# Decoder trunk with expert gathers on one core: three weight buffers, twenty 2 MB weight loads for twenty-three, and a gather ring of eight and then ten rows

## The reference, cut to what matters

```python
for layer in range(2):
    h = rmsnorm(x, norm_mix_g[layer])
    x = x + (hybrid_ab(h, w_in, ..., w_out) if layer == 0 else s5_block(h, ..., glu_w, glu_b))
    h = rmsnorm(x, norm_ffn_g[layer])
    x = x + peer(h, wq[layer], subkeys[layer], u_tab[layer], v_tab[layer])
out = rmsnorm(x, final_norm_g)

def peer(h, wq, subkeys, u_tab, v_tab):          # 8 heads, 128 keys twice, top 16 of 16384 experts
    q = (xt @ wq).reshape(t, 8, 2, 128)
    sc = einsum('thpc,pkc->thpk', q, subkeys)
    sv, si = top_k(sc, 16)                       # both halves, then the best 16 of 16 x 16 pairs
    idx, gate = the 16 best pairs, softmax of their scores
    act = gelu(einsum('td,tkd->tk', x, u_tab[idx]))
    return einsum('tk,tkd->td', gate * act, v_tab[idx])
```

## Time and profile before

| what | value |
|---|---|
| median of 3 runs | 1552.95 us |
| the profiled execution, its own time | 1553.37 us |
| its span | 1551.6 us |
| bytes moved | 603.39 MB, of them 536.90 by the gathers |
| busy, DVE | 1111.5 us (72%) |
| busy, PE | 1097.8 us (71%) |
| busy, ACT | 770.2 us (50%) |

### The profile page before, as it was taken

One profiled execution on the slowest core, in us unless ns is written; L12 is line 12 of the kernel. 1 busy time (PEld: TensorE's weight loads), 2 busy tenths in 40 slices (PEclk: granted clock), 3 DMA queues, 4 the chain that ended last, 5 costly groups with the idle time before them and its releaser, 6 DMA issues.

```text
span 1551.6 us, 19133 instructions
## 1 busy us (share of the span) xinstructions
PE 1097.8 (71%) x5920; PEld 348.4 (22%) x5920; DVE 1111.5 (72%) x2533; ACT 770.2 (50%) x2120; POOL 589.4 (38%) x517
## 2 busy tenths in 40 slices
PE   7997678866765666679866575656878666666665
PEld 3542222322211212223221121212323111111110
DVE  2356887479787899985477799999456866666554
ACT  2315554445456667764334666766334644444433
POOL 0024343323443354554334345344432443434430
PEclk9998689878966776879988567686998777676675
DMA  9569999999999998999999999999999999999995
GB/s 358 179 234 413 420 405 418 414 415 408 415 421 421 354 374 358 410 421 415 412 413 414 403 357 369 355 363 406 380 416 415 415 422 421 421 421 421 421 422 234
DMA packets 105418, 603.39 MB, mean 389 GB/s; under 512 B 9314, under 2 KB 9442, under 8 KB 39780
## 3 DMA queue, kind: packets, MB, share of 16 engines
q0 software_dynamic: 73728, 536.90, 84.8%
q1 hardware_dynamic: 31588, 65.26, 11.3%
HBM read 601.08 MB, written 1.05 MB: 388 GB/s over the span
## 4 chain that ended last, share of the span: by engine, by line
DMA 32%; DVE 31%; PE 22%; ACT 7%; issue 3%; DVEq 3%; ACTq 1%; POOL 1%; SPq 0%; POOLq 0%
DMA rings<-in_uv_tab_dram,idx 24%; DVE rings L1324 11%; PE ps L715 9%; PE ps L920 8%; DMA wst<-in_wq_dram 7%; DVE mem L1231 2%; PE ps L908 2%; DVE dgs L1324 2%; ACT dgs L667 1%; DVE mem L1213 1%; ACT wgt L664 1%; DMA rings<-in_w_in_dram 1%; DVE mem L1242 1%; ACT L661 1%; DVE mem L1240 1%
## 5 line engine op out<-in xcount | busy, mean ns | idle before, releaser
L920 PE MATMUL ps<-rings,dgs 64*64 64x512 f32 x3648 | 638.0, 804 | 343.3 <-ACT dgs L667 342.6
L463 POOL DMA_INDIRECT rings<-in_uv_tab_dram,idx x456 | 521.7, 1144 | 804.3 <-PE ps L920 687.8
L1324 DVE CUSTOM_DVE_ANT_0 rings<-rings,h 128x1024 f32<-128x1024 f32 x456 | 550.7, 1224 | 210.8 <-DMA rings<-in_uv_tab_dram,idx 197.7
L661 ACT ACTIVATE gel<-dots 128x1 f32<-128x1 f32 x512 | 102.1, 199 | 522.2 <-DVE dots L1324 518.5
L920 PEld LDWEIGHTS ps<-rings,dgs 64*64 64x64 f32 x3648 | 128.3, 163 | 783.4 <-ACT dgs L667 682.3
L667 ACT ACTIVATE dgs<-cst,wgt 128x128 f32<-128x128 f32 x512 | 205.6, 402 | 36.3 <-issue 1.5
L715 PE MATMUL ps<-wst,hT 128*128 128x512 f32 x320 | 168.0, 666 | 37.1 <-DMA wst<-in_wq_dram 20.5
L664 ACT ACTIVATE wgt<-gel,share 128x1 f32<-128x1 f32 x512 | 150.8, 295 | 35.5 <-issue 0.3
L920 PE MATMUL ps<-dgs 64*64 64x512 f32 x448 | 80.2, 795 | 53.2 <-ACT dgs L667 53.1
L463 POOL DMA_INDIRECT dgs<-in_uv_tab_dram,idx x56 | 65.9, 1176 | 88.3 <-PE ps L920 74.8
L715 PEld LDWEIGHTS ps<-wst,hT 128*128 128x128 f32 x320 | 63.4, 212 | 138.1 <-issue 134.9
(11 more groups left out here) (192 smaller groups left out, 991.2 us busy)
## 6 DMA issues: line engine op xcount, KB each, us to landing
wst<-in_wq_dram SPq DMA_DIRECT2D x15, 2048.0 KB, 28.2
wst<-in_w_out_dram SPq DMA_DIRECT2D x4, 2048.0 KB, 22.8
wst<-in_glu_w_dram SPq DMA_DIRECT2D x4, 2048.0 KB, 31.7
rings<-in_uv_tab_dram,idx POOLq DMA_INDIRECT x456, 15.7
rings<-in_w_in_dram SPq DMA_DIRECT2D x3, 2048.0 KB, 16.7
rings<-in_w_in_dram SPq DMA_DIRECT2D x2, 1024.0 KB, 7.5
dgs<-in_w_in_dram SPq DMA_DIRECT2D x1, 2048.0 KB, 19.4
vec<-in_vecs_dram SPq DMA_DIRECT2D x3, 512.0 KB, 17.2
```

The costliest lines, as they stand in the source:

```text
L463: nc.gpsimd.indirect_dma_start(out=ring[g % RING], out_offset=None, in_=uv_tab, in_offset=bass.IndirectOffsetOnAxis(ap=idx[n % AHEAD][:, s ...
L661: A.activation(gel[i][:, every], dots[i][:, every], ACT.Gelu_apprx_tanh)
L920: ins = PE.matmul(ps[64 * b:64 * b + 64, 4 + 2 * t + half, :], diag[rows, g % DIAGS, rows], ring[g % RING][rows, D + b * BANK:D + (b + 1) ...
L1324: V.tensor_tensor_reduce(out=u, in0=u, in1=h[:, t, :], scale=1.0, scalar=0.0, op0=ALU.mult, op1=ALU.add, accum_out=dots[n % 2][:, s:s + 1] ...
```

## The change

- A third weight buffer: the whole tile `dgs`, once z (1, 3) has read block 3 of w_in there. `BLOCK_OF` gives the block that each product reads, `BUFFER` the buffer of each block. Both w_out blocks stay in `wst` from tile 0 to tile 1, the first three quarters of wq of layer 0 go one after the other through the third buffer, and the third of them (wq block 2) stays there for both phases. 20 loads are left of 23; layer 1 has the same loads as before, through two buffers.
- `Z_ORDER`: (1, 3) stands sixth, where it stood tenth, and all of it stands in front of `w_mm` of tile 0; half of z 5 stood behind it. The other four products of tile 1 follow later.
- The ring has eight rows, all in `rings`, for g < 80, and ten (two more in `dgs`) from g = 80 on; row 88, the first in `dgs`, waits until the product (1, 2) has left the third buffer.
- Seven diagonals in a tile of their own, `dia`, for 16; ScalarE waits for `v_done` of row g - 7 before it writes one.
- `AHEAD` 8 for 16; the searches of heads 6 to 12 stand four to six slots later; the query quarters of phase 1 stand at slots 68, 74, 81, 89 for 68, 76, 84, 92, and the one of block 2 is now the second.

```diff
-RING = 9
-AHEAD = 16
+SHORT, RING = 8, 10
+SHORT_ROWS = 80
+AHEAD = 8
-DIAGS = 16
+DIAGS = 7
-Q_USE = {(0, 0): 2, (0, 1): 3, (0, 2): 4, (0, 3): 7, (1, 3): 8, (1, 0): 9, (1, 1): 10, (1, 2): 11,
+Q_USE = {(0, 0): 2, (0, 1): 3, (0, 2): 4, (0, 3): 7, (1, 3): 8, (1, 2): 9, (1, 0): 10, (1, 1): 11,
...
-SHARED_USE = 8
+BLOCK_OF = [0, 1, 2, 3, 4, 0, 1, 5, 5, 4, 6, 7] + list(range(8, 20))
+BUFFER = [0, 1, 2, 2, 2, 0, 1, 0] + [1, 0] * 6
...
-Z_ORDER = [(0, 0), (0, 1), (0, 2), (0, 4), (0, 3), (1, 0), (1, 1), (1, 2), (1, 4), (1, 3)]
+Z_ORDER = [(0, 0), (0, 1), (0, 2), (0, 4), (0, 3), (1, 3), (1, 0), (1, 1), (1, 2), (1, 4)]
...
-ROUTE_AT = {1: 0, 2: 16, 3: 26, 4: 40, 5: 50, 6: 72, 7: 80, 8: 88, 9: 96, 10: 104, 11: 112, 12: 120, 13: 134, 14: 150,
+ROUTE_AT = {1: 0, 2: 16, 3: 26, 4: 40, 5: 50, 6: 76, 7: 84, 8: 94, 9: 102, 10: 110, 11: 118, 12: 126, 13: 134, 14: 150,
...
-           ("z", 5, 0, 3), ("mix", 0), ("mix_T", 0), ("mixT_copy", 0), ("z", 5, 3, 4),
-           ("warm",), ("w_mm", 0, 0, 0, 8), ("w_sum", 0, 0), ("w_mm", 0, 1, 0, 8), ("w_sum", 0, 1), ("z", 5, 4, 8),
+           ("z", 5, 0, 4), ("mix", 0), ("mix_T", 0), ("mixT_copy", 0), ("z", 5, 4, 8), ("z_out", 5),
+           ("warm",), ("w_mm", 0, 0, 0, 8), ("w_sum", 0, 0), ("w_mm", 0, 1, 0, 8), ("w_sum", 0, 1), ("z", 6, 0, 4),
...
-    query(0, 76, 1, 0)
-    query(0, 84, 1, 1)
-    query(0, 92, 1, 2)
+    query(4, 10, 1, 2)
+    query(5, 1, 1, 0)
+    query(5, 9, 1, 1)
...
-            for m, ns in ((w_out, (0, 1)), (wq[0], (0, 1, 2)), (w_out, (0, 1)), (wq[0], (3, 0, 1, 2)), (glu_w, (0, 1)),
-                          (wq[1], (0, 1, 2, 3)), (glu_w, (0, 1)), (wq[1], (0, 1, 2, 3))):
+            for m, ns in ((w_out, (0, 1)), (wq[0], (0, 1, 2, 3, 0, 1)), (glu_w, (0, 1)), (wq[1], (0, 1, 2, 3)),
+                          (glu_w, (0, 1)), (wq[1], (0, 1, 2, 3))):
...
+                    earlier = [v for v in range(w) if BUFFER[v] == BUFFER[w]]
+                    if earlier:
+                        last_use = max(u for u in range(len(BLOCK_OF)) if BLOCK_OF[u] == earlier[-1])
                         sp.wait_ge(w_used, last_use + 1)
+                    elif BUFFER[w] == 2:
+                        sp.wait_ge(z_done, Z_ORDER.index((1, 3)) + 1)
...
-                if g < RING and g % 2 == 0:
-                    pool.wait_ge(z_done, 6 + g // 2)
-                if g >= RING:
-                    pool.wait_ge(v_done, g - RING + 1)
+                if g < SHORT and g % 2 == 0:
+                    pool.wait_ge(z_done, 7 + g // 2)
+                if row_ahead(g) >= 0:
+                    pool.wait_ge(v_done, row_ahead(g) + 1)
+                elif ring_at(g) == SHORT:
+                    pool.wait_ge(w_used, Q_USE[1, 2] + 1)
...
+                if g >= DIAGS:
+                    act.wait_ge(v_done, g - DIAGS + 1)
```

More of the change, by code:

```diff
@@ L229, in trunk @@
         wst = sb("wst", [P, 2, KC, BANK])
+        dia = sb("dia", [P, DIAGS * P])
         mem = sb("mem", [P, 9472])
@@ L272, in trunk @@
         sgb = sb("sgb", [P, 8])
-        ring = [rings[:, 2 * D * i:2 * D * (i + 1)] for i in range(8)] + [dgs[:, 2 * D:4 * D]]
+        ring = [w[:, 2 * D * i:2 * D * (i + 1)] for w, rows in ((rings, SHORT), (dgs, RING - SHORT)) for i in range(rows)]
+        weights_in = [wst[:, 0, :, :], wst[:, 1, :, :], dgs[:, :].rearrange("p (k n) -> p k n", k=KC)]
         qs = part(8448, BANK)
@@ L278, in trunk @@
         S = scr[:, :].rearrange("p (g k) -> p g k", g=PH)
-        diag = dgs[:, 0:DIAGS * P].rearrange("p (s t) -> p s t", s=DIAGS)
+        diag = dia[:, :].rearrange("p (s t) -> p s t", s=DIAGS)
         cand = sb("cand", [P, 512])
@@ L317, in trunk @@
         ld_win = [sem(f"ld_win{n}") for n in range(5)]
-        ld_w = [sem(f"ld_w{i}") for i in range(2)]
+        ld_w = [sem(f"ld_w{i}") for i in range(3)]
         ld_vec, ld_col, ld_row = sem("ld_vec"), sem("ld_col"), sem("ld_row")
@@ L359, in bc, with ring_at, ring_turn, row_ahead @@
             return ap.to_broadcast([ap.shape[0]] + [ap.shape[1 + at] if d is None else d for d in dims])
+        def ring_at(g):
+            return g % SHORT if g < SHORT_ROWS else (g - SHORT_ROWS) % RING
+        def ring_turn(g):
+            b = ring_at(g)
+            return sum(ring_at(r) == b for r in range(g + 1))
+        def row_ahead(g):
+            earlier = [r for r in range(g) if ring_at(r) == ring_at(g)]
+            return earlier[-1] if earlier else -1
+        def nth_in(w):
+            return sum(BUFFER[i] == BUFFER[w] for i in range(w + 1))
         def block_of(use):
-            return use - (use >= SHARED_USE)
+            return BLOCK_OF[use]
         def score_cols(p, b):
-            c = 2 * (b if p == 0 else (b + 1) % 4)
+            c = 2 * ((2, 3, 1, 0)[b] if p == 1 else b)
             return slice(c, c + 2)
@@ L458, in _ @@
                     pool.wait_ge(idx_ok, n + 1)
-                if g < RING and g % 2 == 0:
-                    pool.wait_ge(z_done, 6 + g // 2)
-                if g >= RING:
-                    pool.wait_ge(v_done, g - RING + 1)
+                if g < SHORT and g % 2 == 0:
[4 more added lines that the diff above has]
+                    pool.wait_ge(w_used, Q_USE[1, 2] + 1)
                 nc.gpsimd.indirect_dma_start(
-                    out=ring[g % RING], out_offset=None, in_=uv_tab,
-                    in_offset=bass.IndirectOffsetOnAxis(ap=idx[n % AHEAD][:, s:s + 1], axis=0)).then_inc(got[g % RING], 16)
+                    out=ring[ring_at(g)], out_offset=None, in_=uv_tab,
+                    in_offset=bass.IndirectOffsetOnAxis(ap=idx[n % AHEAD][:, s:s + 1], axis=0)).then_inc(got[ring_at(g)], 16)
         @block.scalar
@@ L552, in q_in @@
                 act.wait_ge(w_used, Q_USE[p, b] + 1)
-                act.wait_ge(z_dve, 3 if k == 0 else 4)
+                act.wait_ge(z_dve, 2 if k == 0 else 4)
                 if k > 0:
@@ L562, in q_keep @@
                 if p > 0:
-                    last = cols.stop if p == 1 else PH * (p - 1) + 2 * b + 2
+                    last = {1: cols.stop, 2: 2 * PH, 3: 2 * PH + cols.stop}[p]
                     act.wait_ge(idx_ok, last)
@@ L722, in stream @@
                 if k0 == 0:
-                    pe.wait_ge(ld_w[w % 2], 16 * (w // 2 + 1))
-                product(bank, hTs[t], wst[:, w % 2, :, :], w_used, k0, k1)
+                    pe.wait_ge(ld_w[BUFFER[w]], 16 * nth_in(w))
+                product(bank, hTs[t], weights_in[BUFFER[w]], w_used, k0, k1)
             def norm_T(m):
@@ L907, in glu_mm @@
                 for k in range(k0, k1):
-                    ins = PE.matmul(ps[:, 2 + b, :], hTs[t][:, k, :], wst[:, w % 2, k, :], start=False, stop=(k == KC - 1))
+                    ins = PE.matmul(ps[:, 2 + b, :], hTs[t][:, k, :], weights_in[BUFFER[w]][:, k, :], start=False, stop=(k == KC - 1))
                 if k1 == KC:
@@ L920, in expert @@
                     ins = PE.matmul(ps[64 * b:64 * b + 64, 4 + 2 * t + half, :], diag[rows, g % DIAGS, rows],
-                                    ring[g % RING][rows, D + b * BANK:D + (b + 1) * BANK],
+                                    ring[ring_at(g)][rows, D + b * BANK:D + (b + 1) * BANK],
                                     start=(g % (PH * TOPK) == 0), stop=(g % (PH * TOPK) == PH * TOPK - 1))
@@ L1052, in sgu_var @@
             def sgu_var(t):
[L1054 removed]
+                dve.wait_ge(z_act, (2, 6)[t])
                 g3 = zg[:, t, :].rearrange("p (g d) -> p g d", g=8)
@@ L1321, in dot_product @@
                 n, s, t = g // TOPK, g % TOPK, g // TOPK // PH % T
-                u = ring[g % RING][:, 0:D]
-                dve.wait_ge(got[g % RING], 16 * (g // RING + 1))
+                u = ring[ring_at(g)][:, 0:D]
+                dve.wait_ge(got[ring_at(g)], 16 * ring_turn(g))
                 V.tensor_tensor_reduce(out=u, in0=u, in1=h[:, t, :], scale=1.0, scalar=0.0, op0=ALU.mult, op1=ALU.add,
```

27 lines of the change are left out of this document (12 added, 15 removed).

## The result

The changed kernel takes 1556.57 us, the median of 20 runs (1552.74 to 1559.63); the kernel before, run beside it, 1553.35 us (1550.52 to 1554.72). The ratio is 1.0021, with a 95% interval of 1.0015 to 1.0027: slower, by 3.2 us, just over the 0.2% that the forecast called no change. The forecast was 1545.3 us with a range that ended at 1554.

A forecast was written before the change was run, and what follows sets the result against it. DMA transfers were taken as the bound from 100 to 500 us, VectorE in the S5 stretches. Terms -10.6 + 3.4 + 1.0 + 3.5 - 5.0 = -7.7 us gave 1545.3 us, range 1538 to 1554.

The forecast's parts named there:

- product in front and first rows: Input product ahead of the output product delays row 0, +3.4 us; later z 8 leaves a transfer gap, +1.0 us.
- ring of eight: Up to row 80, one row less in stock costs 2.0 us near row 16 and 1.5 near 200 us: +3.5.
- loads: Three weight blocks not loaded, two of them in the gather stage, at 5.3 us per block: -10.6 us.
- ring of ten: From row 80, a tenth row in hand after each of two VectorE-bound S5 stretches, 2.49 us each: -5.0 us.
- searches four to six slots later: Searches of heads 6 to 12, moved later, are still ahead of their gathers: 0 us.
- So the transfers set the pace there: Claim that DMA transfers bound the stretch from 100 to 500 us, a row costing 2.49 us.
- It can follow if the rows come sooner: Claim that VectorE, waiting 28 times for gathers (35.7 us) in the stretch from 100 to 500, can keep up.
- rival of one buffer: Wq blocks through one buffer come late, TensorE holds back rows and the DMA stands 3.1 us: 1548.4 us, chance 0.02.
- Eight rows eat the gain: Rival: a third place in the ring runs dry, one VectorE stretch gives a row back: -2.7, 1550.3 us, chance 0.19.
- slower: Rival: the eight-row ring runs dry at eight TensorE places before row 88, 19.9 us: +8.7, 1561.7 us, chance 0.09.
- The main item: Sign of being right: from row 0 to the first S5 stretch the time is about 6 us shorter.
- The sign of the slower case: Windows under 400 GB/s at more than four places before 340 us would show the ring running dry repeatedly.

The follow-up runs named there:

- e10: The kernel before with only the new order of the input products (`Z_ORDER` and its place in `PRELUDE`): 1561.13 us, +8.6 against the kernel before.
- e6: The kernel before with eight ring rows up to row 80, then nine: 1558.16 us, +4.1 against the kernel before.
- e13: The changed kernel with both w_out blocks loaded a second time into the buffers that hold them: 1562.89 us, 6.1 us over the changed kernel.
- e5: The kernel before with the three loads that the change removes cut to one eighth of their bytes (wrong weights): 1541.83 us, -12.2 against the kernel before.
- e7: The changed kernel with nine ring rows from row 80 on instead of ten: 1567.30 us, +13.3 against the kernel before.
- e8: The kernel before with seven diagonals, ScalarE's wait for `v_done` and eight index buffers: 1554.20 us, ratio 0.9997 to the kernel before.
- e2: The changed kernel with the searches of heads 6 to 12 at their old slots, phase 1 heads reordered to fit: 1552.10 us, 4.6 us less than the changed kernel.
- e1: The changed kernel with the query quarters of phase 1 eight slots apart again: 1555.06 us, +1.6 against the kernel before.
- e3: The changed kernel with (1, 2), whose output ScalarE makes, as seventh input product: 1552.21 us, 4.5 us less than the changed kernel.
- e4: The changed kernel with old search slots, query quarters eight slots apart and (1, 2) as seventh input product: 1545.41 us, -8.1 against the kernel before.
- e9: The kernel before with eight ring rows up to row 80 and the three loads at one eighth (wrong weights): 1548.07 us, -4.4 against the kernel before.

## Why the prediction was wrong, point by point

| term | forecast, us | measured, us | by |
|---|---|---|---|
| product in front and first rows | +3.4 +1.0 | +8.6 | e10 |
| ring of eight | +3.5 | +4.1 | e6 |
| loads | -10.6 | about -7.7, an estimate | e13, e5 |
| ring of ten | -5.0 | -10.1 | e7 |
| diagonals, ScalarE's wait, index buffers | 0 | +0.2 | e8 |
| searches four to six slots later | 0 | +4.6 | e2 |
| query quarters closer together | not priced | +1.6 | e1 |
| sum | -7.7 | +1.3 | |
| the change | | +3.2 | |

For the loads: w_out twice, -6.1 (e13); of wq block 2 one load less near 340, -4.6 at e5's price, and one that moved out of idle time, +3 at e13's. That sum of -7.7 for the loads is not the forecast's total of -7.7. The measured sum misses the change by 1.9 us; each term has an interval of some 1 to 3 us either way, so the table tells which terms were wrong and not the last microsecond.

- **"The searches of heads 6 to 12 ... are still ahead of their gathers: 0"** is the step that failed most. It asked who needs the result of the moved work (the gathers, much later) and not what stands behind it on its engine. Behind the search of head 12 stood the norm on which the S5 stretch hangs: 5.7 us of search in that chain, 4.6 us of the time (e2).
- **The first rows** were the right mechanism with the wrong size. The output of 2.2 us behind the first search, the start of z 8 near 106 and its wait were all forecast, and came: 4.39 us. The lower clock behind the wait, 1.7 us, was not. And the text then priced only the gap in the transfers, 1.0 us, as if the transfers set the pace from there on. From row 16 to row 60 nothing is won back (8.9 and 9.4 us), nor is it with nine rows (e10 is 7.8 us behind at row 4 and 8.1 at row 60), so what TensorE lost stayed lost: e3 gives back 4.5.
- **The query quarters** at 74, 81 and 89 were named in the list of changes and not followed. A quarter holds its bank for nine slots; seven slots between two of them make TensorE wait with the rows behind it.
- **The loads.** The count was right, two in the stretch that matters and not three, and so was the price in the kernel before (13.9 forecast, 12.2 measured for e5). What failed is "So the transfers set the pace there", said of the whole stretch from 100 to 500, and with it "It can follow if the rows come sooner": only 3 of VectorE's 28 waits lie between 140 and 280, where the w_out loads are removed, and e5 has won 0.7 us by row 60. In the changed kernel the price fell to 3.1 us for each w_out load (e13); that the ring of eight is the reason is likely and not shown.
- **The ring of eight**: 3.5 forecast, 4.1 measured, at the first of the two places named.
- **The ring of ten**: half the size. The two stretches that were counted gave about what was forecast, 5 to 6 us together (e7). Another 3 to 5 us came by row 112, between the query quarters of phase 1, where no S5 stretch lies; why the tenth row pays there no run shows. It hid the errors: without its 5 us above forecast the change would have been 8 us slower.
- **ScalarE's wait for row g - 7: 0** holds, e8. The rival of one buffer did not occur: in the changed kernel TensorE never waits for `dgs` in phase 0.
- **The rivals.** None fits. "Eight rows eat the gain" named ring shortages and 1550.3 us, and "slower" had the ring of eight lose 19.9 us; it lost 4.1 (e6). 11 us lay in three places of the order instead, as e4 shows by taking them out. That e4's 1545.4 meets the forecast of 1545.3 is luck: in it the ring of ten gives twice what was forecast, and the loads give less.

Of what was to show the prediction right, two items came: row 0 near 103.6 (104.23 with the 0.9 of the start) and 597.1 MB. Rows 6 and 7 came at 122.4 for 120, and the S5 stretches moved 366 and 377 GB/s for 368 to 375. The main item failed: from row 0 to row 128 the time was to be some 6 us shorter and is 0.3 us shorter, and to row 136 it is 5.5 us longer. The sign of the slower case came true: windows of ten us from 110 to 340 under 400 GB/s are seven (375, 320, 338, 335, 395, 353 and 376, up to 230), where the kernel before has two. But e6 has five of them and loses only 4.1 us, so their count doesn't give the price.

## What to carry to other kernels

When a table moves a piece of work that nobody waits for yet, look at what stands behind it on the same engine at the new place, above all in front of a stretch that this engine bounds: it is paid there in full. A busy DMA doesn't tell that the rows wait for it: look where the waits for gathers lie, for bytes taken away are felt there and not before. A buffer paid for with ring rows may cost part of that gain too (e9 and e13 lean that way). A wait of TensorE costs more than its length when the clock granted behind it is the lower one: 1.7 us more behind 4.39 here, 2.7 behind 5.70. And if a change bundles several moves and comes out even, measure the parts: here one part was worth -10 us and three slips +11, and mending these made a kernel 0.6% faster out of one 0.2% slower.
